# Memory keys computed between branch B's last projection and the output projection, memory values behind the cross scores

## What is computed

```python
h = rms_norm(x, norm_mix);  z = h @ w_in
oa = moba_attention(qa, ka, va, bias_a) @ w_oa          # branch A: 8 heads of 64
kb, vb = ckv @ w_uk, ckv @ w_uv                         # latent keys and values
ob = dsa_attention(qb, kb, vb, ..., bias_b) @ w_ob      # branch B: 8 heads of 64
ga, gb = sigmoid(z[..., OFF_GA:OFF_GB]), sigmoid(z[..., OFF_GB:])
x = x + (ga * oa + gb * ob) @ w_out
# cross attention to 256 memory tokens, 4 heads of 64
m = rms_norm(mem, mem_norm)
q = rms_norm(x, norm_x) @ wq_x
km, vm = m @ wk_x, m @ wv_x                             # 1024 x 256 weights each
x = x + (softmax(q @ km.T / 8) @ vm) @ wo_x
x = x + hier_moe(rms_norm(x, norm_moe), ...)            # 32 experts, 2 per token
return rms_norm(x, final_norm)
```

## Time and profile before

| | |
|---|---|
| median of three runs | 723.22 us (719.39 to 723.78) |
| the profiled execution: its time | 722.28 us |
| its span, first to last instruction | 720.5 us |
| mean granted TensorE clock | 0.879 |
| PE busy | 518.2 us (72%), 3798 matmuls |
| DVE busy | 203.6 us (28%) |
| ACT busy | 145.0 us (20%) |
| POOL busy | 16.8 us (2%) |
| transferred | 244.21 MB, mean 339 GB/s |
| chain that ended last | PE 48%, DMA 42%, DVE 4%, ACT 3% of the span |

### The profile page before, as it was taken

How to read it: one execution, slowest core, us unless ns; L and a number is a source line. 1 busy time by engine, 2 the same in 40 slices (tenths; PEclk the granted TensorE clock), 3 DMA queues, 4 the chain that set the end, 5 groups by cost and what they waited for, 6 DMA issues and landing times.

```text
span 720.5 us, 8729 instructions
## 1 busy us (share of the span) xinstructions
PE 518.2 (72%) x3798; PEld 328.3 (46%) x3798; DVE 203.6 (28%) x369; ACT 145.0 (20%) x248; POOL 16.8 (2%) x28
## 2 busy tenths in 40 slices
PE   4889999999879799795574474584575448357484
PEld 3789998898779654241131141141123114113121
DVE  4678566276775523010010010010000001001002
ACT  6444456254433422100000000000000000000002
POOL 1200001001000100000000000000000000000001
PEclk9989999999999999898797796798779779679787
DMA  8897533633379597999999999999999999999991
GB/s 288 261 353 256 177 117 117 234 118 117 118 272 409 213 372 270 430 428 427 428 427 430 427 428 429 426 428 427 428 427 429 427 428 428 428 428 427 420 390 74
DMA packets 48217, 244.21 MB, mean 339 GB/s; under 512 B 9072, under 2 KB 18480, under 8 KB 37424
## 3 DMA queue, kind: packets, MB, share of 16 engines
q1 hardware_dynamic: 48176, 243.62, 83.7%
HBM read 242.53 MB, written 4.22 MB: 342 GB/s over the span
## 4 chain that ended last, share of the span: by engine, by line
PE 48%; DMA 42%; DVE 4%; ACT 3%; issue 1%; SPq 1%; POOL 0%; POOLq 0%; PEldq 0%; DVEq 0%; ACTq 0%
PE ps L626 15%; DMA slots_late<-in_w 12%; PE ps L899 10%; DMA slots_own<-in_w 8%; DMA attn_data<-in_w 8%; PE ps L640 6%; PE ps L904 5%; DMA slot_spare<-in_w 4%; DMA slot_last<-in_w 4%; DMA slot_mixed<-in_w 4%; PE ps L608 2%; PE ps L971 1%; PE ps L913 1%; PE ps L561 1%; PE ps L660 1%
## 5 line engine op out<-in xcount | busy, mean ns | idle before, releaser
L899 PE MATMUL ps<-slots_own,x_sb 128*32 128x512 f32 x256 | 97.8, 672 | 20.2 <-DMA attn_data<-in_w 12.4
L899 PE MATMUL ps<-slots_late,x_sb 128*32 128x512 f32 x336 | 81.6, 675 | 41.6 <-DMA slots_own<-in_w 15.9
L405 DVE TENSOR_TENSOR w_low<-slots_own,w_high 128x2048 fp32r<-128x2048 f32 (+1 forms) x33 | 68.0, 2061 | 53.8 <-ACT w_high L1026 53.8
L1536 DVE TENSOR_TENSOR bqT<-ps,bqT 128x512 f32<-128x512 f32 x8 | 5.5, 691 | 237.6 <-ACT bqT L1203 237.6
L899 PE MATMUL ps<-slot_last,x_sb 128*32 128x512 f32 x112 | 61.0, 707 | 10.7 <-DMA slot_spare<-in_w 10.7
L904 PE MATMUL ps<-slots_own,vb 128*32 128x512 f32 x160 | 55.6, 711 | 15.7 <-DMA attn_data<-in_w 7.9
L1200 ACT ACTIVATE vb<-ps 128x256 f32<-128x256 f32 x8 | 3.1, 383 | 311.0 <-PE ps L941 311.0
L626 PE MATMUL ps<-h_high,w_high 128*128 128x256 f32 x224 | 64.8, 289 | 0.0
L626 PE MATMUL ps<-h_low,w_high 128*128 128x256 f32 x224 | 63.7, 284 | 0.0
L626 PE MATMUL ps<-h_high,w_low 128*128 128x256 f32 x224 | 63.6, 284 | 0.0
L1026 ACT ACTIVATE w_high<-slots_own 128x2048 fp32r<-128x2048 f32 (+1 forms) x33 | 56.1, 1700 | 23.4 <-PE ps L640 14.9
(11 more groups left out here) (245 smaller groups left out, 976.0 us busy)
## 6 DMA issues: line engine op xcount, KB each, us to landing
slots_late<-in_w SPq DMA_DIRECT2D x27, 2048.0 KB, 34.9
slots_own<-in_w SPq DMA_DIRECT2D x26, 2048.0 KB, 34.9
attn_data<-in_w SPq DMA_DIRECT2D x18, 2048.0 KB, 33.3
slot_spare<-in_w SPq DMA_DIRECT2D x9, 2048.0 KB, 34.8
slots_own<-in_w_in SPq DMA_DIRECT2D x8, 2048.0 KB, 9.0
slot_last<-in_w SPq DMA_DIRECT2D x8, 2048.0 KB, 36.8
slot_mixed<-in_w SPq DMA_DIRECT2D x8, 2048.0 KB, 32.3
slots_own<-in_w_out SPq DMA_DIRECT2D x2, 2048.0 KB, 7.8
```

The source lines that it names most:

```text
L405: m = eng.tensor_tensor(low, src, high.bitcast(F32), ALU.subtract)
L899: return pe.matmul(ps[SLOTS * e:SLOTS * e + SLOTS, 4 + matrix, :], xeT[:, k, SLOTS * e:SLOTS * e + SLOTS], w, start=(k == 0), stop=(k == K ...
L1536: dve.tensor_tensor(act_sb, ps[:, 5, :].rearrange("p (q f) -> p f q", f=FC), silu_sb.rearrange("p (f q) -> p f q", f=FC), ALU.mult).then_i ...
```

## The change

The keys of the memory (job `km`) move from slot 1 to behind ob3, ahead of out0. The values (job `vm`) move from slot 1 to behind the cross scores, ahead of the transposes of the cross probabilities; their evacuation by ACT stands behind the last cross exponentials, their split behind the transposed parts of the residual. The split memory tokens get memory of their own, `mT_high` and `mT_low`, which lies where `slot_spare` comes later. The slots of the loop are filled anew: ga0 to ga3 in slots 1 and 2, bq in slot 3, gb0 alone in slot 4, gb1 with oa0, gb2 with oa1, gb3 alone, oa2 with oa3. The chunks are regrouped: wk_x comes with wq_x (`kx_qx`, loaded between `ob` and `out0`), wv_x comes with wo_x (`vx_ox`, loaded into slot 6, the memory of the first half of `attn_data`, behind `out1`). The order and the waits of the first 11 expert loads follow from this.

```diff
-MOE_SLOTS = [9, 6, 7, 1, 2, 3, 4, 5, 8, 0, 10]
+MOE_SLOTS = [7, 1, 2, 0, 8, 3, 9, 4, 5, 6, 10]
...
-SLOT_JOBS = [[], ["km", "vm"], ["ga0", "ga1"], ["ga2", "ga3"], ["bq0", "bq1"], ["gb0", "gb1"], ["gb2", "oa0"],
-             ["gb3", "oa1"], ["oa2", "oa3"]]
+SLOT_JOBS = [[], ["ga0", "ga1"], ["ga2", "ga3"], ["bq0", "bq1"], ["gb0"], ["gb1", "oa0"], ["gb2", "oa1"],
+             ["gb3"], ["oa2", "oa3"]]
...
+        with ExitStack() as early:
+            mT_high, mT_low = (early.enter_context(nc.sbuf_tensor(f"mT_{p}", [P, KD, T], F32R)) for p in ("high", "low"))
         slot_spare = sb("slot_spare", [P, SLOT])
...
             def fill(name, parts):
                 c = CHUNKS.index(name)
-                if c >= RING:
+                s = CHUNK_SLOT[c]
+                if s >= RING:
+                    sp.wait_ge(s_read, 8)
+                elif c >= RING:
                     chunk_done(LAST_JOB[CHUNKS[c - RING]])
...
-                if s < RING:
-                    chunk_done(LAST_JOB[[c for i, c in enumerate(CHUNKS) if i % RING == s][-1]])
-                elif s == 8 or s < 6:
+                if s < RING or s == 6:
+                    chunk_done(LAST_JOB[[c for c, slot in zip(CHUNKS, CHUNK_SLOT) if slot == s][-1]])
+                elif s == 3:
                     job_computed(sp, "qx")
-                elif s == 6:
-                    sp.wait_ge(s_read, 8)
+                elif s == 8:
+                    job_computed(sp, "out3")
+                elif s in (4, 5, 9):
+                    job_computed(sp, "vm")
...
             for i in range(4):
                 split_columns(f"ob{i}", oB)
+            split_columns("km", (mT_high, mT_low))
...
                 m.then_inc(xs_done, 1)
+            split_rows("vm", (mT_high, mT_low))
             for h in range(X_HEADS):
                 pe.wait_ge(xprob_set, h + 1)
...
+            job_evacuated(pe, "vm")
             for c in range(2):
                 o = begin(f"ox{c}")
...
             cross_exp(3)
+            copy_job("vm", vm.rearrange("p a b -> p (a b)"))
             cross_copy(2)
```

More of the change, by code:

```diff
@@ L93, in shape_constants @@
     return c, b, np.ascontiguousarray(below)
-JOBS = (["iq", "ikw", "ckv", "ckvT", "aq0", "aq1", "ak0", "ak1", "av0", "av1", "km", "vm"]
+JOBS = (["iq", "ikw", "ckv", "ckvT", "aq0", "aq1", "ak0", "ak1", "av0", "av1"]
         + [f"ga{i}" for i in range(4)]
-        + ["kb0", "kb1", "vb0", "vb1", "bq0", "bq1", "gb0", "gb1", "gb2", "oa0", "gb3", "oa1", "oa2", "oa3"]
-        + [f"ob{i}" for i in range(4)]
-        + [f"out{i}" for i in range(4)] + ["qx", "ox0", "ox1"] + [f"xo{i}" for i in range(4)])
@@ L114 @@
-SPLITS = (["iq", "ikw", "ckv", "aq0", "aq1", "ak0", "ak1", "av0", "av1", "km", "vm"] + [f"ga{i}" for i in range(4)]
-          + ["bq0", "bq1", "gb0", "gb1", "gb2", "oa0", "gb3", "oa1", "oa2", "oa3"]
-          + [f"ob{i}" for i in range(4)] + [f"out{i}" for i in range(4)] + ["qx"])
-SLOT_JOBS = [[], ["km", "vm"], ["ga0", "ga1"], ["ga2", "ga3"], ["bq0", "bq1"], ["gb0", "gb1"], ["gb2", "oa0"],
-             ["gb3", "oa1"], ["oa2", "oa3"]]
+        + ["bq0", "bq1", "kb0", "kb1", "vb0", "vb1", "gb0", "gb1", "oa0", "gb2", "oa1", "gb3", "oa2", "oa3"]
@@ new lines @@
+        + [f"ob{i}" for i in range(4)] + ["km"]
+        + [f"out{i}" for i in range(4)] + ["qx", "vm", "ox0", "ox1"] + [f"xo{i}" for i in range(4)])
+CHUNKS = ["ckv_iq", "aq", "ak", "av", "ga0", "ga1", "bq", "uk_uv", "gb0", "gb1",
+          "oa", "ob", "kx_qx", "out0", "out1", "vx_ox"]
+CHUNK_SLOT = [c % RING for c in range(len(CHUNKS) - 1)] + [6]
+LAST_JOB = {"ckv_iq": "ckv", "aq": "aq1", "ak": "ak1", "av": "av1", "ga0": "ga1", "ga1": "ga3",
+            "uk_uv": "vb1", "bq": "bq1", "gb0": "gb1", "gb1": "gb3", "oa": "oa3", "ob": "ob3", "out0": "out1",
+            "out1": "out3", "kx_qx": "qx", "vx_ox": "xo3"}
@@ new lines @@
+PARTS = {"uk_uv": 2, "kx_qx": 2, "vx_ox": 2}
+assert CHUNK_SLOT[-1] == MOE_SLOTS[-2]
+SPLITS = (["iq", "ikw", "ckv", "aq0", "aq1", "ak0", "ak1", "av0", "av1"] + [f"ga{i}" for i in range(4)]
+          + ["bq0", "bq1", "gb0", "gb1", "oa0", "gb2", "oa1", "gb3", "oa2", "oa3"]
+          + [f"ob{i}" for i in range(4)] + ["km"] + [f"out{i}" for i in range(4)] + ["qx", "vm"])
+SLOT_JOBS = [[], ["ga0", "ga1"], ["ga2", "ga3"], ["bq0", "bq1"], ["gb0"], ["gb1", "oa0"], ["gb2", "oa1"],
+             ["gb3"], ["oa2", "oa3"]]
@@ L132, in landed @@
     c = CHUNKS.index(name)
-    return c % RING, 16 * sum(PARTS.get(CHUNKS[i], 1) for i in range(c % RING, c + 1, RING))
+    s = CHUNK_SLOT[c]
+    return s, 16 * sum(PARTS.get(CHUNKS[i], 1) for i in range(c + 1) if CHUNK_SLOT[i] == s)
 def front_parts(s):
-    return sum(PARTS.get(CHUNKS[i], 1) for i in range(s, len(CHUNKS), RING)) if s < RING else 0
+    return sum(PARTS.get(name, 1) for name, slot in zip(CHUNKS, CHUNK_SLOT) if slot == s)
 def unit_landed(q):
@@ L803, in _ @@
             split_columns("qx", (tT_high, tT_low), h_ready(2))
-            wo = chunk("qx_ox")[:, 2048:4096].rearrange("p (k n) -> p k n", k=2)
-            for name in ("qx", "km", "vm"):
+            wo = chunk("vx_ox")[:, 2048:4096].rearrange("p (k n) -> p k n", k=2)
+            for name in ("km", "qx"):
                 job_evacuated(pe, name)
@@ L1149, in _ @@
                 act.activation(pair(h_high, i), pair(ga, i), ACT.Copy).then_inc(merge_high, 1)
+            copy_job("km", kmT.rearrange("p a b -> p (a b)"))
+            after("km")
             act.wait_ge(small_in, 16 * 7)
             for i in range(4):
-                after(f"out{i}")
+                if i < 3:
+                    after(f"out{i}")
                 if i:
@@ L1155, in _ @@
             split_turned(2, 3, 2, tT_high)
+            after("out3")
             square(x_sb[:, 0, :], 2, 0, xn[:, 0, :], squares[0])
```

50 lines of the change are left out of this document (20 added, 30 removed).

## The result

The changed kernel takes 723.72 us, the median of 20 runs (721.30 to 727.61). The kernel before takes 720.63 us beside it, also over 20 runs (719.07 to 724.58). The ratio is 1.0035 with an interval of 1.0019 to 1.0050: the change makes the kernel slower by 0.35%, some 2.5 us (the medians lie 3.1 us apart). The lowest and the highest of the 20 times lie 2.2 and 3.0 us higher than before, so both ends of the distribution have moved. The predicted 722.8 us is close to the measured time and inside its range, but the forecast was "no change", and that is not what happened: the small loss is real. A second measurement of the same kernel gave 1.0031 (1.0007 to 1.0055).

The account below looks back on a forecast made before the run. The end was taken to hang on when TensorE reaches the expert stage, 85 loads of 4.97 us following. Terms -1.7 -1.2 -0.6 +1.6 +0.8 +1.6 +0 = +0.5 on 722.28 gave 722.8 us, no tellable change; forecast 720.5 to 725, range 718 to 727.

Parts of the forecast that it names:

- Slots 1 to 3, change 0: Loop slots 1 to 3 keep two full jobs each, so the latent projections still end at 129.61: change 0.
- Slot 4, -1.7: Slot 4, gb0 alone, waits for w_oa and its split; slot 5 starts at 142.2 instead of 143.86 us: -1.7 us.
- Slot 5, -1.2 and +1.6 for the clock: Slot 5, one full and one half job, takes 13.09 instead of 14.30 us; slot 4's hole drops the clock, +1.6.
- Slots 7 and 8, -0.6 and +0.8: Slot 7, gb3 alone, saves 0.6 us through slot 8; its 2.9 us TensorE hole is charged +0.8 for the clock.
- Holes and the clock: Idle TensorE stretches above about 2 us drop the clock to 0.50, 1.65 us per drop; new holes charged +1.6 and +0.8.
- Keys behind ob3, +1.6: km ahead of out0 fills a hole and keeps the clock; out1 ends at S + 30.8, not S + 29.2 (S: ob0's start).
- Values behind the scores, 0: vm runs while TensorE waits for cross probabilities; cross output projection at 256.4 us, 0 change, or +2.2 if the clock stays low.
- Loads ahead, 0: Thirteen transfers behind ob3's split; the last lands at 279 us against the 284 needed, 5 us to spare: 0.
- No clock drop in the holes: Rival: the new TensorE holes bring no low clock; sum -1.9, 720.4 us; chance 0.22.
- Removed work is removed time: Rival: ACT and DVE follow, the 11.7 us removed go less km's 1.6; 712.2 us; chance 0.06.
- The low clock stays: Rival: each of two holes costs 6.6 us at half clock, 3.3 lost each; +4.7, 727 us; chance 0.12.
- The loads come late: Rival: loads behind vm, or w_oa, come later and use up the spare 5 us; 728 us; chance 0.06.

Follow-up runs that it names:

- e9: e8 plus matmuls with unused results in slots 7 and 8 and ahead of ob0; 715.77 us, 0.9925 of the kernel before.
- e3: Kernel before plus unused matmuls in its two gaps, within out0 and around the cross probabilities (fillers too long); ratio 1.0070.
- e6: Changed kernel with vm moved right behind km, ahead of out0; ratio 1.0114 to the kernel before.
- e1: Changed kernel plus unused matmuls in its two new holes, slots 4 and 7; ratio 1.0004 to the kernel before.
- e2: Changed kernel with gb0 and gb1 in slot 4, then gb2 with oa0, gb3 with oa1, oa2 alone, oa3 alone; 720.19 us, ratio 0.9989.
- e11: Changed kernel plus unused matmuls in slots 4, 7 and 8 and ahead of ob0; ratio 1.0008 to the kernel before.
- e5: Changed kernel run again unchanged, for a second profile; 724.46 us, ratio 1.0031 to the kernel before.
- e12: Kernel before plus 18 unused matmuls in the gap within out0; ratio 0.9980 to the kernel before.
- e8: Changed kernel with both the two gate jobs in slot 4 (e2) and the exponentials first (e7); 718.47 us, ratio 0.9954 to the kernel before.
- e7: Changed kernel with ACT's last cross exponentials and DVE's last normalising each put ahead of that engine's first cross copy; ratio 1.0019 to the kernel before.
- e10: The same kernel as e8, measured again; 720.33 us, ratio 0.9975 to the kernel before.
- x1: Kernel before, unchanged, profiled again; this execution took 723.94 us.

## Why the prediction was right and wrong

**What bounds it.** Right. In every profile the end followed the first refill by 438.9 to 441.1 us; before, 85 loads took 422.8 us of that. T orders the times in the large (e9 lowest, e3 and e6 highest), but not within 2 us: e1 and e2 are faster than their T says, e11 is slower.

**Slots 1 to 3, change 0.** Right: from the start of slot 1 to the end of the latent projections it is 51.09 us before (78.52 to 129.61) and 51.13 in e5 (79.89 to 131.02).

**Slot 4, -1.7.** Measured -1.9 (12.4 us in place of 14.25, mean of three). The wait for w_oa was forecast at 8.3 us and took 7.5 to 7.9. The idle on TensorE was 3.2 to 3.6 us, not 4.1. With the hole filled slot 4 took 11.74 us in e11, so at full clock the term is -2.5; the missing 0.65 us is the low clock in the weighing, for which I had charged nothing. The second load of the pair, w_ob, landed after 12.2 to 12.5 us: the two landed in order, as in the rows of before. The Trainium skill, "DMA: Bandwidth & Descriptors", section "Two DMAs through the same engine are not ordered", says that the descriptors of a queue start in order and promises no such order for their completion; the landings here agree with the start.

**Slot 5, -1.2 and +1.6 for the clock.** Measured +0.4 together (14.6 to 14.9 us, before 14.30), as forecast. **Slots 7 and 8, -0.6 and +0.8.** Measured +0.3 (22.2 to 22.35, before 21.94), forecast +0.2. The second hole, 2.88 us in the first profile, brought the low clock in all three. So the whole stretch to ob0 is -1.2 where -1.1 was forecast. That the two agree so well is partly luck: with the holes filled (e11) the stretch is 4.3 us shorter than before, so 7.4 of the 11.7 us come back as waits and not 8.2, and the low clock costs 3.1 us there and not 2.4. The picture is right, and two errors of 0.7 to 0.8 us cancel.

**Holes and the clock.** That the low clock costs time on the path is shown (e9, e12: fill the gap, and the drop and its 1.4 to 2.4 us go). The Trainium skill's rule in "TensorE: Matmul & The Clock Gate", Part 1, that activity is what releases the throttle, agrees with both. The drop in out0 costs 1.4 us (11.01 less 9.61), a little less than the 1.65 that I had worked out. What I had wrong is that I read each drop as tied to its gap. The gap of out0 in the kernel before was without a drop in one profile of five; in e8 a gap of 1.86 us had one behind it; with e1's fillers slot 5 was free of it and the ob jobs had one; e2 and e8 are the same program up to ob0 and had two drops and one, 1.6 us apart.

**Keys behind ob3, +1.6.** Measured +2.1 in the mean, and this is part of the miss. The forecast put the end of out1 at S + 30.8, it came at S + 31.0 (222.00 less 0.44 of transposes, less 190.53). The rest is the side of before: S + 29.2 was right to 0.1 us for four executions and 1.4 us too much for the fifth, the one without a drop in out0. And the drop in the old out0 is part of what made km cheap: against e12, where it is filled, km costs 3.2 us (31.40 less 28.23). No idle and full clock between km and out1 were forecast and found (5.98 and 11.52 us).

**Values behind the scores, 0.** This is the step that failed. I let the sum of the parts come out at the old 256.4 and called it nothing, with only one way to be off, the low clock. Measured +0.6 against the usual 20.15 us and +0.7 to 0.8 against the mean of five, 20.0. The clock was 1.00 throughout, so the add-on of 2.2 was not it. The mechanism was as I had it and a size was off: scores and vm end 14.54 us after qx starts, forecast 14.3; and from vm's end to the projection it is 6.22 us, where I had 5.8. In those 5.8 only a copy (0.6) and the last half of the products (0.85) stood behind the last transposes. In the kernel both jobs of products, ox0 and ox1, stand behind the transposes of all four heads, and all 16 matmuls came there, 1.97 us. The row "252.55 3.39 PE ps L828 x16" shows the same in the kernel before, and I read it wrongly.

The ordering that I named myself, the last exponentials behind a copy that waits for vm, was in the forecast with its price, so it does not explain the miss. It is what could have been saved: 1.36 us (e7). Without it the change would have gained 0.6 us here instead of losing 0.8.

**Loads ahead, 0.** Right: the last one was issued at 269.59 and landed 9.7 us later, at 279.3; forecast 279.

**The rivals.** "No clock drop in the holes" did not occur: both holes had one in all three profiles. "Removed work is removed time" is refuted (ob0 at -1.2, not -11.7), but e8 and e2 show that half of its condition, w_oa out of the way, can be had by the order of the jobs: then 3 to 5 us more of the removed work is removed time. "The low clock stays" did not occur in the changed kernel: the most that its 72 matmuls of slot 5 lost was 1.8 us (10.66 less 8.83), not 3.3. "The loads come late" did not occur.

**The number.** The sum +0.5 should have been +1.7, and it was laid on an execution of 722.28 us. The errors of size were small, 0.5 for the keys and 0.7 for the cross attention, both of the same sign. And I set the bar for a change at 1%, 7.2 us, from three runs 4.4 us apart; with 20 runs on each side 0.35% could be told from nothing.

## What to carry over

Work taken off an engine that others are holding up comes back as waits, and whether it returns whole depends on what else stands in the in-order queues: here a load that a projection releases, and an exponential behind a copy. Before a term is halved or quartered, look in the program for where the instructions stand: here all the products stood behind the last transpose. When a piece of work is put under a softmax, go through ACT's and DVE's order for anything that now waits for it; moving one line won back more than the whole placement had lost. And a term that comes out at zero as the sum of seven estimates is not zero: give it an error, of the size of the effect in question.

## What the runs showed of the hardware

A gap of 2.3 to 3.6 us on TensorE is mostly, but not always, followed by a granted clock of 0.50 (out0 of the kernel before: four profiles of five; the two holes of the kernel after: three of three). The 1.64 us in slot 6 was not, and of two gaps of 1.86 us in e8 one was; in e1 a drop came in the ob jobs behind gaps of 1.20 and 0.93 us. The same program shows one drop or two in different executions. A drop costs 1.4 to 2.4 us of work (78 matmuls 11.01 against 9.61 in e12, 72 matmuls 11.37 in e8 against 8.98 in e9). 41 unused matmuls around gaps of under 2 us each (e9) held the clock at 1.00 and were worth 0.3 to 0.5% of the time (against e8 and e10), about as much as the change under study moved.

The first 48 split matmuls of the program take 5.9 or 7.4 to 7.6 us (6.33 once, in e7) from one execution to the next, in both kernels, while the granted clock of the profile reads 1.00 in either (x1 and before, 14 to 23 us). In the profiles with the slow start the low clock behind 40 us also lasts longer, and the latent projections end at 131.0 to 132.0 us, as against 127.6 to 128.8 where both are fast. What decides between them stays open.
